# One fused kernel on Trainium2: in both feed-forward networks the first down projection is computed after the gate and up projections of the 256-wide second chunk

## The chip, the cores and the metric

The kernel runs on one core of one Trainium2 chip. The metric is the device time of one execution in microseconds. The engines are TensorE (PE in the profile, its weight loads PEld), VectorE (DVE), ScalarE (ACT), GpSimd (POOL) and SyncE (SP), which issues the weight DMAs.

## The reference, cut to what matters

Two blocks follow each other on a sequence of 512 tokens of width 1024: two layers of recurrent, latent and memory attention, then a block with two feed-forward networks (FFN) around a mixer. All is in float32. The part that matters here is the network, which occurs twice:

```
def swiglu(x, w_gate, w_up, w_down):      # w_gate, w_up: 1024 x 2816, w_down: 2816 x 1024
    return (jax.nn.silu(x @ w_gate) * (x @ w_up)) @ w_down

f = swiglu(rms_norm(h, pre_g), w_gate, w_up, w_down)
h = h + 0.5 * rms_norm(f, post_g)
```

## The kernel before

**Products.** A float32 operand is split into a high part (rounded to the matmul's fp32r) and a low part (the remainder), and a product is three matmuls: high by high, high by low, low by high. For weights, ScalarE writes the high part (`wh`, line 1417) and GpSimd the remainder (`wl`, line 988).

**Units and buffers.** Weights pass through as units of up to four 128-row tiles. `raw` has two buffers that SyncE fills in the order of the plan (line 969): load r waits until the remainders of load r-2 are written. `wh` and `wl` have three buffers. ScalarE runs two units ahead: with each piece of unit u (`prepare`, lines 1401 to 1418) it makes its share of the tiles of unit u+2, once unit u-1 has been used by TensorE. A piece is the work on one PSUM bank in one unit. ScalarE's queue is strictly in program order: for each piece first `prepare`, then the read of the bank, if it is ScalarE's.

**The network.** `ffn` (lines 643 to 666) cuts the 2816 hidden features into six chunks, 512, 256, 512, 512, 512, 512. For a chunk i let Gi be the gate block (two units, banks 0 to 3, or 0 and 1 for the 256-wide chunk; ScalarE reads the banks with silu into `SG`, line 1438), Ui the up block (the same banks; VectorE multiplies by `SG` into `hidden`, line 1910), Di the down projection of the chunk. D0 to D4 are of the class `Seven`: the 2 x 2 block product (token halves, column halves, halves of the chunk) is computed with seven products in place of eight, in four units, 14 pieces of two row tiles each, on banks 4 to 7. For them VectorE forms
- the sums of the weights (`weight_sums`, line 1871, four instructions) directly in the raw buffers and in `sums`; the first unit of D needs none, the second and third need three, the fourth all four (`source_wait`, line 900);
- the sums and splits of the hidden chunk: `split_first` behind the first half of U's banks (operands a11 and s3), `split_second` behind the last (a12, s1, s2, a22, s4), with the helpers `half_high` (line 1801, a cast), `half_low` (1807, a subtraction) and `combined` (1812). The parts stand in `zh`/`zl` and `yh`/`yl`.

TensorE (`seven_piece`, lines 1048 to 1069) adds one product after another to the banks 6 and 7 (the products 1, 3, 5 and 7) and 4 and 5 (2, 4 and 6), and VectorE reads each piece into `facc` (`read_seven`, lines 1845 to 1858, named L1855 where it copies and L1857 where it adds). A piece waits for the read of the piece that used its bank before it. So the fifth piece of D waits for the read of the first, the ninth for that of the fifth.

**The order.** `plan` is a list that all engines walk: `G0 U0 sums(D0) G1 D0 U1 sums(D1) G2 D1 U2 sums(D2) G3 D2 U3 ...`. sums(D) is an entry for VectorE alone. Behind U0 ScalarE also issues two small DMAs (`load_gains`), for which it waits until U0's banks have been read. D1, of the 256-wide chunk, uses one tile where the others use two. Before its first read of a down projection VectorE waits until ScalarE has read the banks of the gate block ahead of it (`settle_before`).

Of the kernel before, what the change touches and what calls it, by code (L numbers as in the profile page):

```python
# [30 lines left out]
F32 = mybir.dt.float32  # L31
F32R = mybir.dt.float32r
I32 = mybir.dt.int32
U8 = mybir.dt.uint8
ALU = mybir.AluOpType
# [3 lines left out]
P = 128  # L39
SEQ = 512  # L40
D = 1024
T = SEQ // P
# [74 lines left out]
class Seven(Block):  # L117


    def __init__(self, w, ktiles, first):  # L120
        super().__init__(w, ktiles, 512, "seven", "ffv", "seven", "dve", first)
        self.half = ktiles // 2

    def key(self, piece):
        return 4 * piece[1] + piece[2]
# [249 lines left out]
def build(nc, x, x_t, mem_t, positions, w_in, w_uq, w_uk, w_uv, w_mk, w_mv, w_out, ln_g, ln_b, cols_in,  # L375
# [3 lines left out]
    with ctx:  # L379
        def sb(name, shape, dt=F32):  # L380
            return ctx.enter_context(nc.sbuf_tensor(name, shape, dt))
# [16 lines left out]
        side = sb("side", [P, 4096])  # L398
        cols = sb("cols", [P, NCOLS])
        level_mask = sb("level_mask", [P, LEVELS - 1, P // 4], U8)  # L400
        causal = sb("causal", [P, SEQ])
        rope_table, v_n = sb("rope_table", [P, 2, SEQ]), sb("v_n", [P, T, 512])
        work_n, work2_n = 57 * 256, 41 * 256
        with nc.sbuf_tensor("work", [P, work_n], F32) as work:
            pass
# [79 lines left out]
        bank_ready, act_evac, dve_evac = sem("bank_ready"), sem("act_evac"), sem("dve_evac")  # L485
# [8 lines left out]
        def w_cols(w, row0, ktiles, c0, width):  # L494
            return w[row0:row0 + ktiles * P, c0:c0 + width].rearrange("(k p) n -> p k n", p=P)

        plan = []
        add = plan.append
# [54 lines left out]
        for l in range(DEPTH):  # L553
# [10 lines left out]
            for g in range(2):  # L564
# [7 lines left out]
                else:  # L572
                    add(values)
                levels = [Phase("level", pe=4 if level <= LEVELS else 0, act=int(level in (3, LEVELS + 1)),
                                dve=0 if level == 0 else 4 + (level == LEVELS + 1), level=level, slots=2,
# [67 lines left out]
        def ffn(wg, wu, wd, gains, by_columns=False):  # L643

            widths = [512, D_FF % 512] + [512] * (D_FF // 512 - 1)
            chunks = [(sum(widths[:i]), width) for i, width in enumerate(widths)]

            last, seven = len(chunks) - 1, None
            for i, (c, width) in enumerate(chunks):
                add(Block(w_cols(wg, 0, KD, c, width), KD, width, "tr", "x", "silu", "act", SG, banks=width // P))  # L650
                if i:
                    add(Part(seven, 0, 1, 2) if i == last else seven)
                add(Block(w_cols(wu, 0, KD, c, width), KD, width, "tr", "x", "times_gate", "dve", i == last,
                          banks=width // P))
                if i == last:

                    add(Part(seven, 3))
                if i == 0:
                    load_gains(*gains)
                if i < last:  # L660
                    seven = Seven(w_cols(wd, c, width // P, 0, D), width // P, i == 0)
                    add(Sums(seven))
            c, width = chunks[last]
            ends = [Block(w_cols(wd, c, width // P, n * 512, 512), width // P, 512, "nat", "ff", "accumulate", "dve",
                          (n, False)) for n in range(2)]
            norm("post", ends, pre="work2", scale=0.5, by_columns=by_columns)
# [93 lines left out]
        for e in plan:  # L760
# [6 lines left out]
            if isinstance(e, Late):  # L767
                b = e.block
# [98 lines left out]

        def half_parts(s, h):

            return [t[:, s % 4, 0:256 * h].rearrange("p (k t) -> p k t", t=256) for t in ((yh, yl) if s > 2 else (zh, zl))]  # L870


# [895 lines left out]
        def _(dve):  # L1768
# [17 lines left out]
            def after(n):  # L1786

                dve.wait_ge(dve_chain, n)
# [9 lines left out]
            def half_high(name, h):  # L1798

                s = [x[0] for x in SEVEN].index(name)  # L1800
                return noted(dve.tensor_copy(half_parts(s, h)[0], hidden_half(name, h)))

            def half_low(name, h):

                s = [x[0] for x in SEVEN].index(name)
                high_part, low_part = half_parts(s, h)
                dve.tensor_tensor(low_part, hidden_half(name, h), high_part.bitcast(F32), ALU.subtract).then_inc(  # L1807
                    halves_done, 1)

            def combined(name, one, two, op, h):  # L1810

                return noted(dve.tensor_tensor(hidden_half(name, h), hidden_half(one, h), hidden_half(two, h), op))  # L1812

            def split_first(h):
                a11 = half_high("a11", h)
                s3 = combined("s3", "a11", "a21", ALU.subtract, h)
                after(a11)
                half_low("a11", h)
                after(s3)
                s3 = half_high("s3", h)  # L1820
                after(s3)
                half_low("s3", h)
# [51 lines left out]
            def read_bank(pc):  # L1874
                b, _, j = pc
                if b.engine != "dve" or not b.ends(pc):
                    return
                if j == 0 and (b.kind != "seven" or pc[1] == 0):
                    settle_before(dve, b)
                    if b.evac == "times_gate":  # L1880

                        units_over(dve, b.units_before)
                    if b.evac == "residual":
                        dve.wait_ge(x_loaded, 16)
                if b.kind == "seven":
                    read_seven(pc)
                    return
                dve.wait_ge(bank_ready, b.ready[j])
                src = ps[:, b.bank(j), 0:b.width if b.kind == "nat" else SEQ]
                if b.evac == "copy":  # L1890
                    n = min(b.width if b.kind == "nat" else SEQ, b.arg.shape[-1])
                    ins = dve.tensor_copy(b.arg[:, j, 0:n], ps[:, b.bank(j), 0:n])
                elif b.evac == "roped":
                    ins = dve.tensor_tensor(b.arg[:, j, :], src, rope_table[:, j % 2, :], ALU.mult)
                elif b.evac == "residual":
                    n, first = b.arg
                    dst = xs[:, j, n * 512:(n + 1) * 512]
                    ins = dve.scalar_tensor_tensor(out=dst, in0=dst, scalar=ALPHA if first else 1.0,
                                                   in1=src, op0=ALU.mult, op1=ALU.add)
                elif b.evac == "residual_sum":  # L1900
                    n = b.arg[0]
                    dst = xs[:, j, n * 512:(n + 1) * 512]
                    ins = dve.tensor_tensor_reduce(out=dst, in0=src, in1=dst, scale=1.0, scalar=0.0, op0=ALU.add,
                                                   op1=ALU.add, accum_out=stat[:, 32 + 2 * j + n:33 + 2 * j + n])
                elif b.evac == "accumulate":
                    n, first = b.arg
                    dst = facc[:, j, n * 512:(n + 1) * 512]
                    ins = dve.tensor_copy(dst, src) if first else dve.tensor_tensor(dst, dst, src, ALU.add)
                elif b.evac == "times_gate" and not b.arg:
                    dve.tensor_tensor(hidden[:, j, :], src, SG[:, j, :], ALU.mult).then_inc(dve_evac, 1)  # L1910
                    if (j + 1) % (b.banks // 2) == 0:

                        dve.wait_ge(dve_evac, b.evacs[j])
                        if j < b.banks - 1:
                            split_first(b.banks // 2)
                        else:
                            split_second(b.banks // 2)
                    return
                elif b.evac == "times_gate":
                    oh, ol = operand["ff"]  # L1920
                    tmp = hidden[:, j, :]
                    link(dve.tensor_tensor(tmp, src, SG[:, j, :], ALU.mult))
                    link(dve.tensor_copy(oh[:, j, :], tmp))
                    ins = dve.tensor_tensor(ol[:, j, :], tmp, oh[:, j, :].bitcast(F32), ALU.subtract)
                elif b.evac == "merge":
                    n, first, gate = b.arg
                    dst = facc[:, j, n * 512:(n + 1) * 512]
                    if first:
                        ins = dve.tensor_tensor(dst, src, gate[:, j, :], ALU.mult)
                    else:  # L1930
                        tmp = gate[:, j, :]
                        link(dve.tensor_tensor(tmp, src, tmp, ALU.mult))
                        ins = dve.tensor_tensor(dst, dst, tmp, ALU.add)
                ins.then_inc(dve_evac, 1)
# [25 lines left out]
                pending[:] = more  # L1960

            for e in plan:
                if isinstance(e, (Block, Part)):
                    for pc in e.pieces():
                        read_bank(pc)
                        lows_behind(pc)
                    continue
# [519 lines left out]
```

## Time and profile before

| what | value |
|---|---|
| median of 3 runs | 2110.97 us (2109.89 to 2111.05) |
| the profiled execution's own time | 2109.61 us |
| its span | 2107.8 us |
| TensorE busy | 2071.2 us, 98% of the span |
| VectorE, ScalarE, GpSimd busy | 1047.8, 818.4, 945.1 us |
| mean granted TensorE clock | 0.997 |

The first network's D0 begins at 1072.04 us of the span, the second network's at 1736.49 us. Busy times overlap between engines. A matmul's end is modelled and overlaps the next one, so durations of blocks are taken from start to start. "Granted clock" is the share of full speed that TensorE was given. Rows of the table by stage give start and end, the length, then busy us (and instructions) of PE, PEld, DVE, ACT and POOL, the granted clock, the DMA share and GB/s. Timeline rows give start, duration, engine, line, operation, what is written and read, shapes and count; a row is one instruction or a run of equal ones; in brackets stands the idle time before it and what ended it.

### The profile page before, as it was taken

The page shows a single profiled execution, that of the slowest core. Times are in us where ns is not written, and L with a number is a line of the kernel's source. Part 1 is how long each engine was busy: PE and PEld are TensorE (multiplying, and loading weights), DVE is VectorE, ACT ScalarE, POOL GpSimd, SP SyncE. Part 2 cuts the span into 40 slices and gives each one's busy share as a digit, 9 for nine tenths or more (in the row PEclk, how much of TensorE's full clock was granted, in tenths as well). Part 3 has the DMA queues.
Part 4 walks back from the last instruction along what each step waited for, and adds up shares of the span by engine and source line. Part 5 has one row for each costly group of instructions (what it writes and reads, how often), then busy time and mean ns, then how long its engine had stood idle before and what let it go on. Part 6 is the DMA issues. An engine that isn't in the chain of part 4 may idle for free.

```text
span 2107.8 us, 33796 instructions
## 1 busy us (share of the span) xinstructions
PE 2071.2 (98%) x13712; PEld 1723.4 (82%) x13712; DVE 1047.8 (50%) x1861; ACT 818.4 (39%) x1665; POOL 945.1 (45%) x734
## 2 busy tenths in 40 slices
PE   8999999999999999999999999999999998999998
PEld 7878888778978888778877888888888887888886
DVE  6173565525473465535464554533422645534574
ACT  5424335454423335555422323345423422233244
POOL 4633433232443433232365666543444346576533
PEclk9999999999999999999999999999999999999999
DMA  7522223122222223122233323342233133233322
GB/s 248 177 66 81 78 68 100 41 80 81 81 82 70 88 68 94 47 78 73 81 109 111 99 81 100 110 135 81 66 114 100 60 100 100 100 120 100 100 70 90
DMA packets 98685, 196.69 MB, mean 93 GB/s; under 512 B 3681, under 2 KB 12257, under 8 KB 98145
## 3 DMA queue, kind: packets, MB, share of 16 engines
q1 hardware_dynamic: 95072, 183.25, 26.6%
q10 hardware_dynamic: 3456, 11.27, 1.6%
q8 instruction: 109, 1.79, 0.4%
q14 instruction: 48, 0.39, 0.1%
HBM read 192.41 MB, written 2.10 MB: 92 GB/s over the span
## 4 chain that ended last, share of the span: by engine, by line
PE 55%; DVE 3%; ACT 1%; issue 0%; DMA 0%; DVEq 0%; ACTq 0%
PE ps L1038 14%; PE ps L1040 14%; PE ps L1039 14%; PE ps L1066 3%; PE ps L1067 3%; PE ps L1068 3%; PE ps L1179 1%; PE ps L1319 1%; PE ps L1187 0%; PE ps L1196 0%; PE ps L1342 0%; DVE work L1812 0%; PE ps L1362 0%; DVE zl L1807 0%; PE ps L1351 0%
## 5 line engine op out<-in xcount | busy, mean ns | idle before, releaser
L988 POOL TENSOR_TENSOR wl<-raw,wh 128x512 fp32r<-128x512 f32 (+2 forms) x676 | 873.4, 1318 | 1038.5 <-ACT wh L1417 1028.6
L1417 ACT CAST wh<-raw 128x512 fp32r<-128x512 f32 (+2 forms) x692 | 378.5, 604 | 622.4 <-PE ps L1040 436.3
L1038 PE MATMUL ps<-xh,wh 128*128 128x512 f32 (+1 forms) x1376 | 515.0, 374 | 6.7 <-DVE work L1910 5.5
L1040 PE MATMUL ps<-xh,wl 128*128 128x512 f32 (+1 forms) x1376 | 509.5, 370 | 0.0
L1039 PE MATMUL ps<-xl,wh 128*128 128x512 f32 (+1 forms) x1376 | 509.1, 370 | 0.0
L1038 PEld LDWEIGHTS ps<-xh,wh 128*128 128x128 f32 x1376 | 259.7, 189 | 53.0 <-DVE work L1910 6.3
L1040 PEld LDWEIGHTS ps<-xh,wl 128*128 128x128 f32 x1376 | 259.5, 189 | 44.5
L1039 PEld LDWEIGHTS ps<-xl,wh 128*128 128x128 f32 x1376 | 259.7, 189 | 42.2
L1038 PE MATMUL ps<-wh,xh 128*128 128x512 f32 (+1 forms) x608 | 239.0, 393 | 0.2 <-issue 0.2
L1039 PE MATMUL ps<-wl,xh 128*128 128x512 f32 (+1 forms) x608 | 234.3, 385 | 0.0
L1040 PE MATMUL ps<-wh,xl 128*128 128x512 f32 (+1 forms) x608 | 234.3, 385 | 0.0
L1857 DVE TENSOR_TENSOR side<-side,ps 128x512 f32<-128x512 f32 x124 | 84.4, 687 | 127.1 <-PE ps L1068 127.0
L1038 PEld LDWEIGHTS ps<-wh,xh 128*128 128x128 f32 x608 | 114.1, 188 | 22.6 <-issue 1.4
L1040 PEld LDWEIGHTS ps<-wh,xl 128*128 128x128 f32 x608 | 114.1, 188 | 21.7
L1039 PEld LDWEIGHTS ps<-wl,xh 128*128 128x128 f32 x608 | 114.2, 188 | 20.5 <-issue 0.2
L1038 PE MATMUL ps<-wh,yh 128*128 128x512 f32 x304 | 123.3, 405 | 0.9 <-ACT work L1440 0.7
L1040 PE MATMUL ps<-wh,yl 128*128 128x512 f32 x304 | 118.8, 391 | 0.0
L1039 PE MATMUL ps<-wl,yh 128*128 128x512 f32 x304 | 118.6, 390 | 0.0
L988 POOL TENSOR_TENSOR wl<-work,wh 128x512 fp32r<-128x512 f32 x54 | 71.8, 1350 | 99.4 <-ACT wh L1417 98.8
L1910 DVE TENSOR_TENSOR work<-ps,work 128x512 f32<-128x512 f32 x36 | 24.8, 688 | 175.3 <-PE ps L1040 175.3
L1417 ACT CAST wh<-work 128x512 fp32r<-128x512 f32 x54 | 32.1, 617 | 146.7 <-DVE work L1871 99.7
L1438 ACT ACTIVATE work<-ps 128x512 f32<-128x512 f32 x76 | 45.7, 601 | 68.4 <-PE ps L1040 68.3
(296 smaller groups left out, 2985.0 us busy)
## 6 DMA issues: line engine op xcount, KB each, us to landing
raw<-w_in SPq DMA_DIRECT2D x58, 1024.0 KB, 5.2
raw<-w_out SPq DMA_DIRECT2D x20, 1024.0 KB, 5.0
raw<-f1g SPq DMA_DIRECT2D x10, 1024.0 KB, 5.2
raw<-f1u SPq DMA_DIRECT2D x10, 1024.0 KB, 5.1
raw<-f1d SPq DMA_DIRECT2D x10, 1024.0 KB, 5.1
raw<-f2g SPq DMA_DIRECT2D x10, 1024.0 KB, 5.1
raw<-f2u SPq DMA_DIRECT2D x10, 1024.0 KB, 5.1
raw<-f2d SPq DMA_DIRECT2D x10, 1024.0 KB, 5.0
```

Of the source, the lines that this page charges most:

```text
L988: pool.tensor_tensor(wl[s], source(u, k), wh[s].bitcast(F32), ALU.subtract).then_inc(low_done, 1)
L1038: pe.matmul(o, still[0], move[0], start=k0 + k == 0, stop=False)
L1039: pe.matmul(o, still[0], move[1], start=False, stop=False)
L1040: mm = pe.matmul(o, still[1], move[0], start=False, stop=k0 + k == b.ktiles - 1)
L1066: pe.matmul(o, sh, mh, start=k == 0 and s in CHAIN_FIRST, stop=False, skip_group_check=True)
L1067: pe.matmul(o, sh, ml, start=False, stop=False, skip_group_check=True)
L1068: mm = pe.matmul(o, sl, mh, start=False, stop=k == h - 1, skip_group_check=True)
L1179: mm = pe.matmul(ps[:, 4 + h, 0:width], q_heads[:, 2 * p + h, cut], k_heads[:, p, h, 0:width], start=True, stop=True)
L1417: act.copy(wh[:, v % 3, k, 0:width], source(v, k)).then_inc(high_done, 1)
L1438: ins = act.activation(b.arg[:, j, :], src, ACT.Silu)
L1857: ins = dve.tensor_tensor(dst, dst, src, ALU.add)
L1910: dve.tensor_tensor(hidden[:, j, :], src, SG[:, j, :], ALU.mult).then_inc(dve_evac, 1)
```

## The change

In both networks the plan becomes `G0 U0 G1 sums(D0) U1 D0 sums(D1) G2 D1 U2 ...`; from G2 on the order is the same. U1's reads no longer split anything; VectorE splits chunk 1 behind the bank reads of D0: a11 after the second read, s3 after the fourth, the rest after the fourteenth. The operands of chunk 1, the only one with halves of one tile, go to the new tensors `few_h` and `few_l` in place of `zh`/`zl` and `yh`/`yl`; they take the space of three tensors of the first block (`causal`, `rope_table`, `v_n`), which are 3584 words per partition as they are.

```diff
-        self.half = ktiles // 2
+        self.half, self.turn_over = ktiles // 2, False
...
-        causal = sb("causal", [P, SEQ])
-        rope_table, v_n = sb("rope_table", [P, 2, SEQ]), sb("v_n", [P, T, 512])
+        with (nc.sbuf_tensor("causal", [P, SEQ], F32) as causal, nc.sbuf_tensor("rope_table", [P, 2, SEQ], F32) as rope_table,
+              nc.sbuf_tensor("v_n", [P, T, 512], F32) as v_n):
+            pass
+        few_h, few_l = sb("few_h", [P, 7, 256], F32R), sb("few_l", [P, 7, 256], F32R)
...
-            last, seven = len(chunks) - 1, None
+            last = len(chunks) - 1
+            sevens_of = [Seven(w_cols(wd, c, width // P, 0, D), width // P, i == 0) for i, (c, width) in enumerate(chunks[:-1])]
             for i, (c, width) in enumerate(chunks):
                 add(Block(w_cols(wg, 0, KD, c, width), KD, width, "tr", "x", "silu", "act", SG, banks=width // P))
-                if i:
-                    add(Part(seven, 0, 1, 2) if i == last else seven)
+                if i == 1:
+
+                    add(Sums(sevens_of[0]))
+                elif i:
+                    add(Part(sevens_of[i - 1], 0, 1, 2) if i == last else sevens_of[i - 1])
                 add(Block(w_cols(wu, 0, KD, c, width), KD, width, "tr", "x", "times_gate", "dve", i == last,
                           banks=width // P))
                 if i == last:
 
-                    add(Part(seven, 3))
+                    add(Part(sevens_of[i - 1], 3))
                 if i == 0:
                     load_gains(*gains)
-                if i < last:
-                    seven = Seven(w_cols(wd, c, width // P, 0, D), width // P, i == 0)
-                    add(Sums(seven))
+                if i == 1:
+                    sevens_of[0].turn_over = True
+                    add(sevens_of[0])
+                if 0 < i < last:
+                    add(Sums(sevens_of[i]))
...
         def half_parts(s, h):
 
+            if h == 1:
+                return [t[:, s:s + 1, :] for t in (few_h, few_l)]
...
+            def split_a11(h):
+                after(half_high("a11", h))
+                half_low("a11", h)
+
+            def split_s3(h):
+                after(combined("s3", "a11", "a21", ALU.subtract, h))
+                after(half_high("s3", h))
+                half_low("s3", h)
...
                     dve.tensor_tensor(hidden[:, j, :], src, SG[:, j, :], ALU.mult).then_inc(dve_evac, 1)
+                    if b.banks == 2:
+
+                        return
...
             for e in plan:
+                if isinstance(e, Seven) and e.turn_over:
+
+                    for pc in e.pieces():
+                        read_bank(pc)
+                        if pc[0].key(pc) == 1:
+                            dve.wait_ge(dve_evac, e.evac_before[1])
+                            split_a11(1)
+                        elif pc[0].key(pc) == 3:
+                            split_s3(1)
+                    split_second(1)
+                    continue
```

## Rows read from the trace of the kernel before

**Rows 1.** The page: busy us, share and instructions; the chain that ended last.

```profile
PE 2071.2 (98%) x13712; PEld 1723.4 (82%) x13712; DVE 1047.8 (50%) x1861; ACT 818.4 (39%) x1665; POOL 945.1 (45%) x734
PE 55%; DVE 3%; ACT 1%; issue 0%; DMA 0%; DVEq 0%; ACTq 0%
```

**Rows 2.** Busy time by stage: D0, G2, U2 with G3, D2, second network's D0 and G2.

```profile
1072.04:1096.04 24.00, 21.07 (x85) 16.89 (x84) 14.33 (x19) 8.93 (x20) 17.61 (x17) 0.93 0.23 66
1106.94:1131.80 24.86, 22.05 (x98) 17.93 (x97) 11.86 (x22) 4.07 (x7) 7.32 (x6) 1.00 0.20 64
1141.47:1185.08 43.61, 43.61 (x194) 35.96 (x193) 22.29 (x28) 11.76 (x22) 28.88 (x22) 1.00 0.38 121
1185.08:1204.39 19.31, 19.31 (x85) 15.77 (x84) 8.93 (x13) 8.18 (x15) 14.40 (x12) 1.00 0.22 63
1736.49:1760.51 24.02, 21.10 (x85) 16.83 (x84) 14.33 (x19) 8.92 (x20) 17.62 (x17) 0.93 0.23 69
1771.41:1797.79 26.38, 23.68 (x98) 19.09 (x96) 11.75 (x22) 4.07 (x7) 7.21 (x6) 0.94 0.19 60
```

**Rows 3.** TensorE's timeline at G1's start and at three stops.

```profile
1061.15 0.39 PE L1038 MATMUL ps<-xh,wh 128*128 128x512 f32 x1
...
1080.72 0.76 PE L1066 MATMUL ps<-wh,zh 128*128 128x512 f32 x1 [2.92 <-DVE side L1855]
...
1112.61 0.50 PE L1038 MATMUL ps<-xh,wh 128*128 128x512 f32 x1 [2.81 <-DVE work L1910]
...
1776.97 0.75 PE L1038 MATMUL ps<-xh,wh 128*128 128x512 f32 x1 [2.70 <-DVE work L1910]
```

**Rows 4.** VectorE's timeline in the first network.

```profile
1075.24 2.47 DVE L1871 TENSOR_TENSOR work<-raw,work 128x1024 f32<-128x1024 f32 x2
1079.93 1.29 DVE L1855 COPY side<-ps 128x512 f32<-128x512 f32 x2 [2.21 <-ACT work L1438]
...
1104.50 0.69 DVE L1910 TENSOR_TENSOR work<-ps,work 128x512 f32<-128x512 f32 x1 [7.57 <-PE ps L1040]
1105.22 1.17 DVE L1801 CAST zh<-work 128x256 fp32r<-128x256 f32 x1
1106.31 1.51 DVE L1812 TENSOR_TENSOR work<-work 128x256 f32<-128x256 f32 x1
1107.74 1.52 DVE L1807 TENSOR_TENSOR zl<-work,zh 128x256 fp32r<-128x256 f32 x1
1109.19 1.37 DVE L1801 CAST yh<-work 128x256 fp32r<-128x256 f32 x1
...
1111.88 0.68 DVE L1910 TENSOR_TENSOR work<-ps,work 128x512 f32<-128x512 f32 x1
...
1113.13 0.29 DVE L1801 CAST yh<-work 128x256 fp32r<-128x256 f32 x1
1113.33 0.42 DVE L1812 TENSOR_TENSOR work<-work 128x256 f32<-128x256 f32 x1
1113.67 0.42 DVE L1807 TENSOR_TENSOR zl<-work,zh 128x256 fp32r<-128x256 f32 x1
```

**Rows 5.** ScalarE's timeline in the first network.

```profile
1076.49 1.14 ACT L1417 CAST wh<-work 128x512 fp32r<-128x512 f32 x2 [11.16 <-DVE work L1871]
...
1079.05 0.59 ACT L1438 ACTIVATE work<-ps 128x512 f32<-128x512 f32 x1
...
1088.13 1.33 ACT L1417 CAST wh<-raw 128x256 fp32r<-128x256 f32 x4 [5.38 <-PE ps L1068]
```

**Rows 6.** GpSimd's timeline in the first network.

```profile
1089.98 2.84 POOL L988 TENSOR_TENSOR wl<-raw,wh 128x256 fp32r<-128x256 f32 x4
...
1098.69 12.99 POOL L988 TENSOR_TENSOR wl<-raw,wh 128x512 fp32r<-128x512 f32 x10 [1.80 <-ACT wh L1417]
```

**Rows 7.** The page's DMA issues: count, KB each, median us to landing.

```profile
raw<-f1d SPq DMA_DIRECT2D x10, 1024.0 KB, 5.1
```

## The prediction

> **What bounds the kernel now.** I read the page's engine line first: TensorE is busy for 2071.2 us of a span of 2107.8 us, and the chain of waits is TensorE with 3% of VectorE in it [rows 1]. So nearly every microsecond that can be had is one in which TensorE stands still or runs at its lower clock, and an edit outside its queue counts only by such stretches. Second, the table by stage, with the stages cut at the first matmul of each block [rows 2]. G, U and D are the gate, up and down blocks of a chunk. An undisturbed D of a 512-wide chunk (D2, its 84 matmuls) takes 19.31 us, and an undisturbed pair of U and G (192 matmuls) 43.61 us, so a G alone takes 21.80 us. D0 takes 24.00 us in the first network and 24.02 in the second; G2 takes 24.86 and 26.38 us. Against the undisturbed blocks that is 4.69, 4.71, 3.06 and 4.58 us lost: 17.0 us in all, and both blocks stand on either side of the 256-wide U1, which the change moves.
>
> Third, TensorE's timeline at these four places [rows 3]. In D0 the fifth piece (the first that accumulates onto a bank already written) starts 2.92 us late, waiting for VectorE's first bank read (L1855). Behind the stop the granted clock falls: it averages 0.93 over D0 where D2 has 1.00 [rows 2], so some 24 x 0.07 = 1.7 us go to the lower of the two levels (1.2 GHz for 2.4), and 2.92 + 1.7 is the loss of 4.7 again. In G2 the second piece starts 2.81 us late (2.70 in the second network), waiting for VectorE's read of U1's second bank (L1910); in the second network the clock falls behind it too (0.94, and 1.5 us more are lost), in the first it does not (1.00).
>
> Fourth, VectorE's timeline says why it is late [rows 4]. Between the end of U0 (1061.15 us) and D0 (1072.04) there is only G1, 10.9 us. In it VectorE reads U0's last bank, splits hidden chunk 0 until 1073.0, then forms the four weight sums until 1077.7. ScalarE waits 11.16 us for those sums with the weights of D0's second unit, has its reads of G1's banks queued behind them (the second at 1079.05) [rows 5], and VectorE waits another 2.21 us for the second of these. The other stop: VectorE reads U1's first bank at 1104.50, spends 1105.22 to 1111.9 on five split operations, and only then reads the second bank, which G2 needs.
>
> Those operations are slow for a reason that the timelines show side by side: while GpSimd computes weight remainders (1098.69 to 1111.68, 1.30 us each) the 256-wide VectorE operations start 1.09, 1.43, 1.45 and then 1.35 us apart; with GpSimd idle they start 0.20 (a cast) and 0.34 us (a subtraction) apart [rows 4, 6]. Reads of PSUM take 0.69 us either way.
>
> **The change part by part.** (1) The order G1, D0, U1, G2 becomes G1, U1, D0, G2, in both networks. No matmul is added or removed. Between U0 and D0 TensorE now has G1 and U1, 21.8 us, so D0 begins at 1061.15 + 21.80 = 1082.95 [rows 3]. VectorE's splits for chunk 0 end by 1073, earlier if anything, since the remainders that GpSimd computes beside them are now four 256-wide ones of 0.71 us [rows 6]. Cover 10 us: cost nothing.
>
> (2) The weights of D0 come after those of U1 in SyncE's queue. The first 1 MB half waits for U1's first remainders (1063.8 + 2.8 = 1066.7) and lands 5.1 us later [rows 7], at 1071.9. The second half waits for U1's last remainders: ScalarE makes their high parts only around its read of G1's first bank, which is full at 1061.15 + 5.45 + 2.72 = 1069.3 (G1 is half a G, four equal pieces); read 0.6, two copies 0.33 each, two remainders 0.71 each [rows 5, 6] gives 1072.0, landing 1077.1. The weight sums need both halves. The first meets a wide remainder of D0's first unit (GpSimd 1072.8 to 1078.1) and ends near 1079.3, the others take 1.2 each [rows 4]: third at 1081.7, fourth at 1082.9.
>
> (3) What queues behind the sums: on ScalarE the high parts of D0's second unit (from 1081.8; GpSimd's remainders follow, the first at 1084). D0 wants them at 1082.95 + 4 x 1.38 = 1088.5 (a piece of D0 is 19.31 / 14 = 1.38 us). Cover 4.5 us. On VectorE U1's two bank reads wait for the sums: 1082.9 to 1084.3, just ahead of D0's first full bank at 1084.3. TensorE doesn't want U1's banks (0 and 1) before G2, 19 us on, and D0 uses banks 4 to 7. G1's banks must be emptied before U1: the first at 1069.9 (wanted 1072.04), the second at 1072.8 (wanted 1074.8). So the first stop goes, and the second too: before G2 nothing but reads that are 19 us old is wanted. This returns the 17.0 us.
>
> (4) The splits of chunk 1 now stand between D0's bank reads: two operations behind the second read, three behind the fourth, eleven or so after the last. GpSimd then computes D0's second to fourth unit and G2's without a break (ten remainders of 1.3 us from 1082.9, then eight), so they run at the slow pace. Reads 1 and 2 end at 1086.4. By the spacing of the nearest rows, the same 256-wide operations just after a bank read, a11 costs 1.09 + 1.43 = 2.5, to 1088.9; reads 3 and 4 (0.69 each) to 1090.3; s3 costs 1.09 + 1.43 + 1.45 = 4.0, to 1094.3; read 5 ends at 1095.0, and TensorE starts 0.1 later. The ninth piece, which accumulates on that bank, is due at 1082.95 + 8 x 1.38 = 1094.0. Stop: 1.1 to 1.2 us a network. The reads after it catch up at 0.69 against 1.38. Bounds: at the fast pace (0.20 and 0.34) nothing is late; with every operation at 1.52, the longest of its size [rows 4], read 5 ends at 1096.0 and the stop is 2.1 us, and if the clock falls behind it, as it did after three of the four longer stops, 1.7 us more: 3.8. I take 1.2, the value of the nearest rows, and no fall of the clock.
>
> This slow pace is where a page bears. The Trainium skill, "SBUF — State Buffer", section "Who interferes with whom": VectorE's instructions with two SBUF inputs, or in a two-port mode, and GpSimd's share a pair of ports as an exclusive lock, and the loser waits for the other's whole instruction. The trace agrees in kind [rows 4, 6]. If every one of the five found a GpSimd operation just begun, each would pay 1.3 + 0.2 to 0.34, the stop would be 2.4 us, and the sum 12.2 instead of 14.6.
>
> (5) The rest of chunk 1's splits: eleven and more operations from 1104.8, some four at the slow pace until GpSimd's last ready remainder, near 1108.5, the others 0.3 each, ending near 1112; sums of D1 (half as wide as D0's 1.2 us ones, so 0.6 each) until 1115. Wanted by D1 at 1082.95 + 19.31 + 1.2 + 21.8 = 1125.3. Cover 10 us. ScalarE's read of G2's first bank is at 1117. G2's own weights: the second half is asked for when the remainders of D0's third unit are done (about 1093.3), lands at 1098.4, and its own remainders end at 1106.4; G2's second unit starts at 1114.
>
> (6) The operands of chunk 1 go to tensors of their own, laid over three that the networks don't use; as many bytes, no instruction. Nothing.
>
> Sum: 17.0 - 2 x 1.2 = 14.6 us off the profiled execution's 2109.61 (span 2107.8 and 1.8 around it): 2095.0. The median of the runs shown lies 1.36 higher, so I predict 2096.4.
>
> **Rivals.** A, no new stop: the five operations slip between GpSimd's, or the order of issue favours VectorE. For it: the pace depends on phase, and the stop is only 1.2 us past the cover. Time 2111.0 - 17.0 = 2093.9. B, the new stop is long, about 2 us, and the lower clock follows it: 17.0 - 2 x 3.8 = 9.4, time 2101.6. For it: three of four stops were followed by it; against: those were 2.7 us and more. C, the moved waits bite: the second half of D0's weights lands late (one queue, two gain loads beside it), the sums and D0's second unit follow, and TensorE stops there. The cover is 4.5 us; each further microsecond is one lost in each network. At 3 us past the cover, with the clock falling behind the stop, this gives 17.0 - 2 x (1.2 + 3 + 1.7) = 5.2, time 2105.8. D, the same mechanism on the other side: if the landing slips by 14 us, 9.5 past the cover, the loss per network is 9.5 + 1.7, 22.4 in all, against 17.0 returned: slower by 5.4, 2116.4. It decides from 6.8 us past the cover (6.8 + 1.7 = 17.0 / 2). Against it: the ten landings of this kind have a median of 5.1 us [rows 7]. E, the stops only move: G2 waits in its turn for the VectorE reads of D0. Against it: different banks.
>
> **Chances.** Forecast 0.55, A 0.17, B 0.14, C 0.08, D and everything on the slower side 0.04, E or no change 0.02. Faster than 0.2% (4.2 us, about what this measurement can tell) holds the forecast, A, B and most of C: 0.94; same 0.03; slower 0.03. Range: from A with the lowest run shown, 2092.5, to B, 2101.5.
>
> **What would show it.** Right: D0 ends near 1103.5 and G2 takes 21.8 us with no wait above 0.3; the weight sums start near 1077 and end near 1083; one short TensorE stop in D0, before its ninth piece, for a VectorE read behind the s3 split, with the split operations at 1.1 to 1.5 us; TensorE's granted clock 1.0 throughout D0 and G2. Wrong: a stop before D0's fifth piece for GpSimd's remainders (C), a stretch at 0.5 clock (B), or a D0 above 22 us.

## The result, and the profile after

The changed kernel takes 2094.27 us (median of 4 runs, 2092.51 to 2095.32) where the kernel before took 2110.43 (median of 4): ratio 0.9924, interval 0.9912 to 0.9937, so 16.2 us less. The forecast was 2096.4 us. The profiled execution took 2095.08 us with a span of 2093.2.

The table by stage of the changed kernel, cut at the first matmuls of D0, G2 and again D0, G2 in the second network:

```profile
core 0: us, PE busy (x) PEld busy (x) DVE busy (x) ACT busy (x) POOL busy (x), PEclk, DMA share, GB/s
1085.49:1104.81 19.32, 19.32 (x86) 15.77 (x85) 15.14 (x21) 9.04 (x17) 19.32 (x15) 1.00 0.33 109
1104.81:1126.58 21.77, 21.77 (x98) 18.02 (x97) 12.21 (x18) 4.07 (x7) 9.94 (x8) 1.00 0.30 97
1742.30:1761.62 19.32, 19.32 (x86) 15.77 (x84) 15.62 (x21) 9.32 (x18) 19.08 (x15) 1.00 0.34 109
1761.62:1783.39 21.77, 21.77 (x98) 18.02 (x97) 12.48 (x18) 4.07 (x7) 10.40 (x8) 1.00 0.31 97
```

D0 takes 19.32 us twice, what D2 took in the kernel before, and G2 21.77; the granted clock is 1.00 in all four [rows 2]. That is 4.68 + 3.09 + 4.70 + 4.61 = 17.1 us back. TensorE has no wait between 1072 and 1140 us of the span, nor between 1720 and 1800.

The profiled execution lost only 14.5 us against 2109.61, because its first network begins late: D0 starts at 1085.49, which with 21.8 us of G1 and U1 before it puts G1's start at 1063.7 against 1061.15 [rows 3]. These 2.5 us lie ahead of the networks: 1.7 us of them in the first 300 us of the span, where TensorE's waits for GpSimd's weight remainders add up to 10.5 us against 8.8. They aren't tied to the new order. The kernel of the first experiment below keeps the old order, waits 10.5 us there too and starts D0 1.6 us late; in the kernels below that have the new order, D0's start lies between 1082.71 and 1085.53 us. What decides it was not looked into. That the span's difference is 14.6 us, the forecast's own sum, is an accident of this.

VectorE's timeline answers to [rows 4]:

```profile
1080.07 2.39 DVE L1890 TENSOR_TENSOR work<-raw 128x1024 f32<-128x1024 f32 x1 [4.49 <-DMA raw<-f1d]
1082.38 1.21 DVE L1890 TENSOR_TENSOR raw<-raw 128x1024 f32<-128x1024 f32 x1
1083.51 2.47 DVE L1890 TENSOR_TENSOR work<-raw,work 128x1024 f32<-128x1024 f32 x2
1085.90 1.28 DVE L1929 TENSOR_TENSOR work<-ps,work 128x512 f32<-128x512 f32 x2
1087.58 0.69 DVE L1874 COPY side<-ps 128x512 f32<-128x512 f32 x1 [0.40 <-DVE work L1929]
1088.49 0.69 DVE L1874 COPY side<-ps 128x512 f32<-128x512 f32 x1 [0.22 <-PE ps L1078]
1089.10 0.70 DVE L1811 CAST few_h<-work 128x256 fp32r<-128x256 f32 x1
1089.83 1.41 DVE L1817 TENSOR_TENSOR few_l<-work,few_h 128x256 fp32r<-128x256 f32 x1
1091.16 1.27 DVE L1876 TENSOR_TENSOR side<-side,ps 128x512 f32<-128x512 f32 x2
1092.36 0.41 DVE L1822 TENSOR_TENSOR work<-work 128x256 f32<-128x256 f32 x1
1092.80 1.28 DVE L1811 CAST few_h<-work 128x256 fp32r<-128x256 f32 x1
1094.11 1.41 DVE L1817 TENSOR_TENSOR few_l<-work,few_h 128x256 fp32r<-128x256 f32 x1
1095.44 2.47 DVE L1874 COPY side<-ps 128x512 f32<-128x512 f32 x4
```

The weight sums wait for the load of D0's second half, as computed; the first of them takes 2.39 us beside a GpSimd operation. Then come U1's two reads, D0's first two reads, a11 in two operations (1089.10 to 1091.16), two reads, s3 in three (1092.36 to 1095.44), and the fifth read, which ends at 1096.1. D0's ninth piece starts at 1096.64, without a wait. Where a piece is held up by a bank read in these kernels, it restarts 0.7 to 0.8 us after that read's start (0.78 at the ninth piece), so this one could have started at 1095.44 + 0.78 = 1096.2. The margin is 0.4 us here and 0.2 in the second network (1753.3 against 1753.46). Two of the five split operations, the first behind each pair of reads, took 0.73 and 0.44 us from start to start (1.01 and 0.44 in the second network), the other three 1.31 to 1.33.

GpSimd's timeline over the same stretch, for [rows 6]:

```profile
1066.19 6.21 POOL L998 TENSOR_TENSOR wl<-raw,wh 128x256 fp32r<-128x256 f32 x6 [9.79 <-ACT wh L1427]
1073.13 1.90 POOL L998 TENSOR_TENSOR wl<-raw,wh 128x256 fp32r<-128x256 f32 x2 [0.72 <-ACT wh L1427]
1076.33 5.04 POOL L998 TENSOR_TENSOR wl<-raw,wh 128x512 fp32r<-128x512 f32 x4 [1.30 <-ACT wh L1427]
1085.45 5.50 POOL L998 TENSOR_TENSOR wl<-work,wh 128x512 fp32r<-128x512 f32 x4 [4.08 <-ACT wh L1427]
1090.91 5.75 POOL L998 TENSOR_TENSOR wl<-raw,wh 128x512 fp32r<-128x512 f32 x4
```

Without a break from 1085.45 on it works on D0's later units; the wide remainders take 1.38 to 1.44 us in the mean of a row beside the splits.

ScalarE's, for [rows 5]: it still waits for the weight sums (6.94 us), but no read of G1's banks is queued behind that wait now. Both were done (1072.16, 1074.80) before it began.

```profile
1072.16 0.60 ACT L1448 ACTIVATE work<-ps 128x512 f32<-128x512 f32 x1 [2.03 <-PE ps L1050]
...
1074.80 0.60 ACT L1448 ACTIVATE work<-ps 128x512 f32<-128x512 f32 x1 [1.44 <-PE ps L1050]
...
1084.76 2.18 ACT L1427 CAST wh<-work 128x512 fp32r<-128x512 f32 x4 [6.94 <-DVE work L1890]
```

### The profile page after: what moved, and what is told of

The parts are those of the page before. It is cut to its first block, busy times and chain, and to the rows that moved or that the text cites. A ratio compares the mean times of both kernels' runs of the same rounds, so it can differ in the third digit from the quotient of the medians.

```text
span 2093.2 us, 33796 instructions
## 1 busy us (share of the span) xinstructions
PE 2066.5 (99%) x13712; PEld 1720.9 (82%) x13712; DVE 1055.7 (50%) x1861; ACT 818.8 (39%) x1665; POOL 949.7 (45%) x734
## 4 chain that ended last, share of the span: by engine, by line
PE 57%; ACT 1%; DVE 1%; DMA 0%; issue 0%; DVEq 0%; ACTq 0%
PE ps L1048 15%; PE ps L1050 15%; PE ps L1049 15%; PE ps L1077 3%; PE ps L1076 3%; PE ps L1078 3%; PE ps L1189 1%; PE ps L1329 1%; PE ps L1197 0%; PE ps L1206 0%; PE ps L1352 0%; PE ps L1372 0%; PE ps L1361 0%; PE ps L1242 0%; PE ps L1224 0%
```

## The experiments

Nine runs follow. The theory: both stops were queues on VectorE (and, in D0, on ScalarE behind it) and the new order takes them out of TensorE's way, while the moved splits fit between D0's reads by a narrow margin. The rivals are named with each.

**The stop in G2 alone.** In the kernel before, only the second read of U1 is moved ahead of the splits:

```diff
+                    if b.banks == 2:
+                        if j == 1:
+                            dve.wait_ge(dve_evac, b.evacs[j])
+                            split_first(1)
+                            split_second(1)
+                        return
                     if (j + 1) % (b.banks // 2) == 0:
```

> The kernel before with one edit: U1's two bank reads come first, all splits of chunk 1 behind them; the order G1, D0, U1, G2 and D0's place stay. Theory: the stop in G2 came only from the second bank read queued behind five split operations at the slow pace, so G2 takes 21.8 us in both networks and the kernel gains 3.06 + 4.58 = 7.6 us (ratio 0.9964, about 2102.8 us); D0 keeps its 24.0 us. Rival: it is GpSimd's slow pace as such that matters, and 18 operations behind the reads, eight of them slow, push the sums of D1 and ScalarE's reads of G2's banks late: then TensorE stops later in G2 or in D1 and less than 4 us are gained.

Measured: 2101.92 us (5 runs), ratio 0.9957 (0.9945 to 0.9970). D0 and the stretch of G2 in both networks:

```profile
1073.64:1097.43 23.79, 20.86 (x85) 16.69 (x84) 14.33 (x19) 8.92 (x20) 17.60 (x17) 0.93 0.22 63
1108.33:1130.09 21.76, 21.76 (x98) 18.01 (x97) 11.66 (x23) 4.07 (x7) 7.36 (x6) 1.00 0.23 75
1734.74:1758.74 24.00, 21.07 (x85) 16.86 (x84) 14.34 (x19) 8.92 (x20) 17.62 (x17) 0.93 0.24 68
1769.64:1791.39 21.75, 21.75 (x97) 18.00 (x96) 11.52 (x23) 4.07 (x7) 7.22 (x6) 1.00 0.23 74
```

G2 is whole in both networks and D0 loses what it lost before. So about half of the gain (8.3 of 16 us by the medians, 7.7 by these stages) is to be had without moving D0 at all: one bank read had stood behind five operations that nobody was waiting for yet.

**The changed kernel again,** on the same chip as the others:

> The changed kernel as it is, beside the others on one chip. Theory: both stops gone in both networks and no new one: 17.0 us less, ratio 0.9920. Rival, the stop that the prediction had put before D0's ninth piece is there in part of the executions: then 14.6 to 17 us and D0 between 19.3 and 20.5 us.

Measured: 2094.49 us (4 runs), ratio 0.9919 (0.9905 to 0.9932); D0 19.32 and 19.34 us. The stop that had been predicted is in neither of the two profiled executions, in neither network. Here the margin before the ninth piece is 0.7 us in the first network and 0.1 in the second.

**The new order without the new place of the splits.** All 18 operations directly behind U1's reads:

```diff
+                    dve.wait_ge(dve_evac, e.evac_before[1])
+                    split_a11(1)
+                    split_s3(1)
+                    split_second(1)
                     for pc in e.pieces():
                         read_bank(pc)
-                        if pc[0].key(pc) == 1:
-                            dve.wait_ge(dve_evac, e.evac_before[1])
-                            split_a11(1)
-                        elif pc[0].key(pc) == 3:
-                            split_s3(1)
-                    split_second(1)
```

> The changed order G1, U1, D0, G2, but all 18 split operations of chunk 1 directly behind U1's reads, ahead of D0's first bank read. Theory: VectorE begins D0's reads some 16 to 22 us after D0's start (ten to eighteen operations at 1.3 us beside GpSimd) where the fifth piece wants the first at 5.5 us; TensorE stops for 10 to 16 us in each network and runs at the lower clock behind it (1.5 to 1.8 us more). Against the changed kernel 23 to 35 us worse, so slower than before by 6 to 18 us: 2117 to 2129 us. Rival: the order alone brings the gain and the place of the splits hardly matters: below 2105 us.

Measured: 2121.26 us (4 runs), ratio 1.0047 (1.0033 to 1.0061), slower than before. TensorE's restarts in D0, and the two D0:

```profile
1100.29 0.77 PE L1076 MATMUL ps<-wh,zh 128*128 128x512 f32 x1 [11.29 <-DVE few_l L1817]
...
1770.66 0.77 PE L1076 MATMUL ps<-wh,zh 128*128 128x512 f32 x1 [11.90 <-DVE few_l L1817]
```

```profile
1083.24:1115.52 32.28, 20.99 (x86) 16.77 (x84) 24.80 (x34) 8.82 (x17) 20.25 (x16) 0.84 0.22 73
1753.00:1786.79 33.79, 21.89 (x85) 17.46 (x84) 25.42 (x34) 9.42 (x18) 20.54 (x16) 0.80 0.21 69
```

The new order with all splits ahead of D0's reads is a loss of 11 us; the edit on VectorE's queue is the other half of the change.

**All splits behind D0's last read:** the same edit, with the four added lines behind the loop.

> The changed kernel with all splits of chunk 1 behind D0's fourteenth read, none between. Theory: the place between the reads cost nothing and gave nothing; D0 stays 19.3 us, the chunk's splits and D1's weight sums end 4 to 6 us later than in the changed kernel (near 1121 us of the span), which ScalarE's reads and D1 still don't feel: ratio to before as that of the changed kernel, 0.992. Rival: D1's second unit or ScalarE's reads of G2's banks come late behind the sums and TensorE stops before G3 or in D1: 2 to 6 us worse than the changed kernel.

Measured: 2094.68 us (5 runs), ratio 0.9922 (0.9908 to 0.9935). D0 19.32, G2 21.77, D1 9.80 us: nothing is late. The expected end of D1's sums (1121 us) was wrong: they end at 1115.1, 32.4 us after D0's start against 31.8 in the changed kernel. From about 1108.5 on, with GpSimd out of ready weights, the operations take 0.3 us each, wherever they stand in the queue. This form is as fast, and doesn't hang on a margin of 0.1 to 0.7 us.

**The stop in D0 alone.** In the kernel before, D0's four weight sums are copies; the subtraction is left out:

```diff
+                    if b.arg:
+                        if n:
+                            dve.wait_ge(sums_done, 4 * b.place + n)
+                        dve.tensor_copy(weight_half(b, SUMS[n]), weight_half(b, one)).then_inc(sums_done, 1)
+                        continue
```

> The kernel before, in which the four weight sums of D0 alone are copies of their first operand (the subtraction is left out), which should take 0.6 us each for 1.2. Theory: the stop in D0 came from the chain splits, sums, ScalarE's queue, VectorE's wait, so it shrinks by the 2.4 us that the sums get shorter, from 2.92 to 0.5 us, and the clock doesn't fall: D0 19.5 to 20 us for 24.0, G2 unchanged, about 2102 us. Rival: the stop comes from the weights' remainders on GpSimd or from the loads: D0 stays at 24 us.

Measured: 2106.69 us (8 runs), ratio 0.9988 (0.9975 to 1.0000). D0 takes 21.20 and 21.56 us with the clock at 1.00, and the restart is

```profile
1079.42 0.47 PE L1066 MATMUL ps<-wh,zh 128*128 128x512 f32 x1 [1.65 <-issue]
...
1078.63 1.29 DVE L1855 COPY side<-ps 128x512 f32<-128x512 f32 x2 [2.68 <-ACT work L1438]
...
1075.18 1.14 ACT L1417 CAST wh<-work 128x512 fp32r<-128x512 f32 x2 [9.89 <-DVE work L1874]
```

The profile puts the stop down to "issue", but it is the same wait: the restart comes 0.79 us after the start of VectorE's first bank read, as in the kernel before (1080.72 and 1079.93). The stop shrank less than expected, by an error of mine that the trace settles. ScalarE goes on after the third sum, not the fourth, and the copies start 0.7 to 0.8 us apart, so ScalarE begins at 1075.18 for 1076.49 [rows 5], 1.31 us earlier. D0 begins at 1072.01, where it began before (1072.04). The stop shrinks from 2.92 to 1.65 us, 1.27 less: one for one. In the second network ScalarE is 1.28 us earlier too, counted from D0's start, but VectorE follows its read 0.35 us later than before, and the stop shrinks to 2.00 us; that 0.35 us is not explained. The clock doesn't fall behind either of the shorter stops. G2 was expected unchanged and was not: the clock fell behind its stop of 2.90 us in the first network and not behind that of 2.32 us in the second, the other way round from the kernel before. With 4.0 us by the medians the gain is half of the 8 to 9 us expected; the two D0 give 5.3 us in the profiled execution.

**Why the predicted stop didn't come: the phase against GpSimd.** s3 one read earlier:

```diff
-                        elif pc[0].key(pc) == 3:
+                        elif pc[0].key(pc) == 2:
                             split_s3(1)
```

> The changed kernel with the s3 split behind the third bank read in place of the fourth: one read between the two splits where there were two. Theory (the predicted stop did not come because two bank reads, 1.2 us, last as long as one GpSimd operation, 1.3 us, so that the first split operation behind them finds the port just free and takes 0.44 us): here the first operation behind one read meets the middle of a GpSimd operation and its start-to-start time is 0.9 to 1.3 us; D0 has no stop or one below 0.5 us, since only the fourth read is late. Rival (an operation with two SBUF inputs behind a read slips in whatever the phase): 0.4 to 0.5 us again.

Measured: 2097.28 us (3 runs), ratio 0.9938 (0.9898 to 0.9978). VectorE after a11, with one read before s3:

```profile
1088.53 0.67 DVE L1876 TENSOR_TENSOR side<-side,ps 128x512 f32<-128x512 f32 x1
1089.13 0.92 DVE L1822 TENSOR_TENSOR work<-work 128x256 f32<-128x256 f32 x1
1090.09 1.26 DVE L1811 CAST few_h<-work 128x256 fp32r<-128x256 f32 x1
```

The subtraction takes 0.96 us from start to start for 0.44 (0.96 in the second network too), and stops of 0.63 and 0.84 us appear before D0's eighth piece, which waits for the fourth read (D0 20.23 and 20.45 us). I had put them below 0.5. With three runs the interval overlaps that of the changed kernel; here, and with one extra sum below, it is the stages that tell the two apart, not the medians.

**Five in a row.** a11 and s3 both behind the fourth read:

```diff
-                        if pc[0].key(pc) == 1:
+                        if pc[0].key(pc) == 3:
                             dve.wait_ge(dve_evac, e.evac_before[1])
                             split_a11(1)
-                        elif pc[0].key(pc) == 3:
                             split_s3(1)
```

> The changed kernel with the a11 and the s3 split both behind the fourth bank read. Theory: the five run in a row at about 1.33 us (the first 0.4 to 1.1), from 6.2 us after D0's start to 11.9 to 12.6; the fifth read ends at 12.6 to 13.3 and the ninth piece, due at 11.04, starts 1.7 to 2.4 us late: D0 21 to 21.7 us without a fall of the clock, up to 23.4 with one. Rival: the margin is larger than the trace lets one think, and D0 stays at 19.3.

Measured: 2099.53 us (5 runs), ratio 0.9951 (0.9928 to 0.9973). Stops of 1.70 and 2.00 us before the ninth piece; the clock falls behind the second:

```profile
1083.05:1104.35 21.30, 19.60 (x86) 15.69 (x84) 15.87 (x21) 8.93 (x17) 20.23 (x16) 1.00 0.38 120
1741.88:1765.05 23.17, 21.18 (x85) 16.82 (x84) 16.54 (x21) 9.26 (x18) 20.28 (x16) 0.93 0.36 114
```

**The margin, by doses.** The first weight sum of D0 computed once more (in the second kernel four times more), with the rest unchanged:

```diff
+                    if b.arg and n == 0:
+                        for _ in range(1):
+                            link(dve.tensor_tensor(sums[:, 0, 0:b.half, :], weight_half(b, one), weight_half(b, two),
+                                                   ALU.subtract))
```

> The changed kernel with the first weight sum of D0 computed twice: everything on VectorE behind it comes 1.2 us later. Measured cover in the changed kernel: the fifth read ends 10.6 us after D0's start, the ninth piece is due at 11.04: 0.45 us; D0's second unit of weights 4.1 us. Theory: a stop of 0.5 to 1.2 us before the ninth piece in each network, D0 19.8 to 20.5 us. Rival: the lock with GpSimd resets the phase and takes the delay up: D0 19.3 us.

Measured: 2095.53 us (3 runs), ratio 0.9940 (0.9914 to 0.9966); D0 19.97 and 20.53 us with stops of 0.40 and 0.96 us before the ninth piece. 1.2 us of delay cost 0.65 and 1.21 us of D0, less in the network that had the larger margin. (D0 loses 0.2 to 0.3 us more than a stop's figure; 0.16 of that is because the idle time is counted from the modelled end of a matmul, 0.39 us behind its start, where the next one would have started after 0.23.)

> The changed kernel with the first weight sum of D0 computed five times: everything on VectorE behind it, and ScalarE's high parts of D0's second unit, come 4.8 to 5.2 us later. Theory (the only covers in D0 are 2.7 us for the first read, due 5.5 us after D0's start and ending at 2.8, and 0.45 us for the fifth): first bank read ends at 7.6 to 8, a stop of 2.1 to 2.5 us before the fifth piece, and a second of 2 to 3 us before the ninth, behind the a11 and s3 splits: D0 23.5 to 25 us without a fall of the clock, 25 to 26.7 with one, about 2103 to 2109 us. Nearly the loss of the kernel before (24.0) is back. Rival: VectorE catches up between the reads and only the first stop remains: D0 below 22.5 us.

Measured: 2106.05 us (10 runs), ratio 0.9978 (0.9969 to 0.9988): two thirds of the gain are gone. D0 takes 26.33 and 25.30 us. Its stops in the first network, with VectorE's first bank read and GpSimd's remainders of D0's second unit:

```profile
1091.15 0.47 PE L1076 MATMUL ps<-wh,zh 128*128 128x512 f32 x1 [1.86 <-POOL wl L998]
...
1094.67 0.47 PE L1076 MATMUL ps<-wh,yh 128*128 128x512 f32 x1 [0.48 <-issue]
...
1100.06 0.76 PE L1076 MATMUL ps<-wh,yh 128*128 128x512 f32 x1 [2.40 <-DVE few_l L1817]
...
1090.35 1.29 DVE L1874 COPY side<-ps 128x512 f32<-128x512 f32 x2 [0.40 <-DVE work L1933]
...
1088.23 5.46 POOL L998 TENSOR_TENSOR wl<-work,wh 128x512 fp32r<-128x512 f32 x4 [9.13 <-ACT wh L1427]
```

The profile puts the first stop down to GpSimd's remainders, whose second ends at 1091.13, just before the restart. But the fifth piece begins with a tile whose remainder was done at 1089.90, and it restarts 0.80 us after the start of VectorE's first read, in the second network too (1754.63 and 1755.43), in line with the 0.73 to 0.79 of the other stops for a read. So this is VectorE's read, as expected. With sums 5 us late the cover of D0's second unit is gone as well, but behind that longer wait: the piece was due 5.60 us after D0's start, at 1089.12, its first remainder is 0.8 us late and its second, wanted at 1089.82, 1.3. In the second network the stops are 2.37 us before the fifth piece and 1.62 before the ninth.

And here the first operation of s3, again behind two reads, did not slip in:

```profile
1093.89 1.27 DVE L1876 TENSOR_TENSOR side<-side,ps 128x512 f32<-128x512 f32 x2
1095.09 1.56 DVE L1822 TENSOR_TENSOR work<-work 128x256 f32<-128x256 f32 x1
1096.68 1.26 DVE L1811 CAST few_h<-work 128x256 fp32r<-128x256 f32 x1
```

## Why the prediction was right, and where not

**The stops and their worth** (17.0 us): right. Measured 17.1 by the stages of the profiled executions (3.1 and 4.6 in the two G2, 4.7 in each D0) and 16.2 by the medians. The first experiment separates them. That the 1.5 to 1.8 us at the lower clock behind a stop would go with the stop was right too: the clock is 1.00 in all four blocks.

**The chain behind D0's stop** (splits, sums, ScalarE's queue, VectorE's wait): right, and shown by the copied sums, 1.31 us earlier and 1.27 us less stop in the first network (1.28 and 0.92 in the second). A shorter chain, without ScalarE's queue (sums, U1's reads, D0's first read), can be made to bite in the changed kernel: 5 us more of sums bring D0 to 25 and 26 us.

**The timing of the weight sums**: right to half a microsecond. Counted from D0's start the first sum was to begin at -5.9 and began at -5.4, the fourth to end at 0 and ended at +0.5. One row under it was mis-read, with no effect: I took 0.71 us for a 256-wide remainder from a stretch in which VectorE only read banks. Beside the splits of chunk 0 it takes 1.03 us (6.21 for six): the two engines slow each other. So those splits did not end "earlier if anything" but as long after U0 as before, 11.9 us.

**The new stop of 1.2 us per network**: wrong; there is none. The failed term is "s3 costs 1.09 + 1.43 + 1.45 = 4.0" and, less, "a11 costs 1.09 + 1.43 = 2.5". Measured 3.08 and 2.06 us (3.07 and 2.33 in the second network). The fifth read ended 10.6 us after D0's start, not 12.05: 0.9 us of that is s3, 0.5 a11, 0.2 the third and fourth read, which start 0.6 us apart and not 0.69; the splits began 0.2 us later than forecast, which takes as much back. The ninth piece wants it at 11.15; the 11.04 of the prediction is eight times the mean piece, and D0's first six pieces take 1.40 us each.

The error is that a row taken behind one read was used behind two. A 256-wide VectorE operation from SBUF to SBUF waits for the GpSimd remainder that is under way, while a bank read lasts 0.69 us beside GpSimd as without it. In the changed kernel a remainder begins 0.25 us before the two reads, the reads last 1.20 us and that remainder 1.47, so VectorE comes back just as GpSimd changes over. In all four cases of the two profiled executions of this kernel its subtraction got in first (0.44 us from start to start), and in both with one extra sum. With one read between it came in the middle and took 0.96. With four extra sums it came behind the same two reads and lost in both networks (1.59). The two kinds of case in GpSimd's single rows, in the changed kernel (VectorE's subtraction starts at 1092.36) and with four extra sums (1095.09):

```profile
1092.38 1.55 POOL L998 TENSOR_TENSOR wl<-raw,wh 128x512 fp32r<-128x512 f32 x1
...
1095.07 1.30 POOL L998 TENSOR_TENSOR wl<-raw,wh 128x512 fp32r<-128x512 f32 x1
```

In all eight cases the two operations are recorded as starting within 0.02 us of each other. In the six, VectorE's takes 0.41 us and GpSimd's 1.55 to 1.58; in the two, GpSimd's takes 1.28 and 1.30 and VectorE's 1.56. What decides this race stays open; the recorded starts don't tell it, since in one of the six GpSimd's is 0.02 us ahead as well. A lost race costs 1.15 us, more than the margin of 0.1 to 0.7. So the rival A of the prediction, without a new stop, is what happened, and a stop of 0.4 to 1.0 us, an estimate from these numbers, is one lost race away.

The time came out 2.1 us below the forecast, about the 2.4 us put on the two new stops that were not there.

The page "SBUF — State Buffer" of the Trainium skill (section "Who interferes with whom") says that whoever issues first gets the shared ports for its whole instruction. These runs agree: the first of a group takes 0.36 to 1.59 us from start to start depending on where in the other's instruction it arrives, those behind it 1.31 to 1.33 in the changed kernel and 1.30 to 1.55 with five in a row. The prediction's worst case by that rule, every operation a full wait, was still further off than the rows.

**The rivals.** What happened is A. B, the low clock behind the new stop, can be produced: it came behind a stop of 2.00 us in the kernel with five in a row. C, D0's weights late, bit in no run. With the sums 4.8 us later the second unit's remainders are 0.8 and 1.3 us late in the first network, so the cover was 3.4 to 4.0 us where the prediction had 4.5, and there VectorE's first read is later still. The prices of C and D were not added up alike: C's sum has the new stop of 1.2 us in it and D's has not.

## What to carry to other kernels

A bank read that the matrix engine will want soon belongs ahead of operand preparation that is wanted later; moving one read past five operations gave half of this gain. When work is moved between reads of a chain, price each group by how its first operation meets the other engine's instruction, and not by one average pace. Of two equally fast places take the one that doesn't hang on a margin of tenths of a microsecond: here the splits behind the last read. And where the profile names the releaser of a wait, compare the restart with the other things the instruction waits for: the one named was the wrong one at the first stop with four extra sums.

## What the runs showed of the hardware that was not expected

- 256-wide GpSimd subtractions take 0.71 us beside bank reads and 1.03 us beside 512-wide VectorE operations from SBUF to SBUF; 512-wide ones 1.26 and up to 1.44 in the mean of a row, and a single one up to 1.58 where VectorE got in first.
- The granted clock of TensorE (1.00 is 2.4 GHz, the lower level 1.2) did not fall behind any stop up to 1.86 us in D0 or G2 of these kernels. Behind longer ones it went either way. In D0 it fell behind one of 2.00 us (0.93 over the block), and behind 2.37, 2.40, 2.92, 2.93 and 11 to 12 us, but not behind another of 2.00 in the kernel with copied sums. In G2 it fell behind 2.70 and 2.90 us and not behind 2.32 and 2.81.
- D1 takes 9.79 us where it took 9.67, with the same 42 matmuls; its operands stand in other tensors now. With the splits behind the last read it takes 9.80, with the old order and the old tensors (the first experiment) 9.67. Which of the two changes makes it was not tried.
